# Expert weights loaded in 4 MB pieces of 32 KB per partition, with contraction rows in order 8p+c

## The chip, the cores and the metric

The kernel runs on one core of one Trainium2 chip. The metric is the device time of that core in microseconds (us). All arithmetic is in float32. The engines named below are TensorE (PE, with its weight loads PEld), VectorE (DVE), ScalarE (ACT), GpSimd (POOL) and SyncE (SP). SP issues nearly all loads; they run on 16 DMA engines that the queues of SP and ACT share.

## The reference, cut to what matters

Two transformer blocks are computed on 256 tokens of width 1024. The first ends in a mixture of 32 experts, of which each token takes 4. Each expert has three matrices of 1024x1024 floats (4 MB each), and every one is read once: 32 x 3 x 4 MB is 403 MB of the 537 MB that the kernel reads.

```python
def expert_block(args):
    xe, e = args
    gate = jnp.minimum(xe @ w_gate[e] + b_gate[e], SWIGLU_LIMIT)
    up = jnp.clip(xe @ w_up[e] + b_up[e], -SWIGLU_LIMIT, SWIGLU_LIMIT)
    act = (up + 1) * (gate * jax.nn.sigmoid(SWIGLU_ALPHA * gate))
    return act @ w_down[e] + b_down[e]
```

Ahead of it stand a modulation (`h * (1 + scale) + shift`, whose shift and scale come from `silu(c) @ w_ada + b_ada`), attention and a router. The second block (three kinds of attention and a dense feed-forward) follows it.

## The kernel before

**Places for weights.** Weights stand in SBUF in slots of 4096 words per partition (16 KB, 2 MB over 128 partitions). Six of them are the tensor `ring`. In the expert stage two more, in `arena` (words 13312 on), make it a rotation of `MRING = 8`, and one block (`ASIDE`, number 3) has a place of its own once. `moe_ring`, `moe_block` and `moe_loaded` (L417 to L433) give slot and semaphore of a block.

**Blocks.** A matrix of an expert is two blocks, its halves by contraction rows. In a block, partition p holds four rows that stand together in memory: `block_load` (L531) reads rows 512 x half + 4p + c. So one load of 2 MB is 128 pieces of 16 KB, each contiguous at both ends. There are 192 blocks: 32 experts x 3 matrices x 2. `weight_block` (L449) numbers the 24 blocks of a group of four experts in the order in which they are used: gate(1), up(1), down(0), gate(2), up(2), down(1), gate(3), up(3), down(2), gate(4), down(3), up(4), where 4 is the first expert of the next group. The last group ends with down(3).

**Loads.** All are issued on SP, in order of use. `first_loads` (L550) brings the blocks 0 to 13 of the first group; those in `EARLY` (9 to 13) come in halves of 1 MB (8 KB per partition), each when a half of a block before it has been read. `expert_load` (L536) brings the rest: for each half SP waits until TensorE has used the block whose slot comes free (`X["used"]`), then issues 2 MB.

**TensorE.** `halves` (L2304) waits for a block's load and then does 8 matmuls, four chunks c of contraction rows times two halves g of the 512 output columns, into the two 64-partition halves of one bank. A float32 matmul is two instructions, so a block is 16 rows of the profile at L2318. `w[:, c, 512 * g:512 * g + 512]` is the moving operand, 512 words in one run. The stationary operand is the gathered tokens (`xeT`) or the turned activations (`actT`). So that chunk c of `xeT` holds rows 512 x half + 4p + c, the normed tokens are turned back in that order by `turn_back` (L2244) into `hperm`, and the modulation's shift for them (parts 6 and 7 of `w_ada`) is gathered with a step of 4 (`mod_transpose` and `mod_sums`, L1972 and L1981).

**A group.** `group_pe` (L2408) runs gate, up and down of each expert with the turning of activations (`act_transpose`, L2358), the gather of the next group's tokens (`gather`, L2294) and the combination into the residual (`combine`, L2379) between. `last_expert` does the last down and combine. The second block's weights follow on the same SP queue.

Of the kernel before, what the change touches and what calls it, by code (L numbers as in the profile page):

```python
# [17 lines left out]
ACT = mybir.ActivationFunctionType  # L18
AX = mybir.AxisListType

P = 128
# [78 lines left out]
def two_blocks(nc, t, out):  # L100
    ctx = ExitStack()
    with ctx:
# [160 lines left out]
        hperm = area(1024, 2048).rearrange("p (t h c d) -> p t h c d", t=TT, h=2, c=4)  # L263
# [148 lines left out]

        def moe_place(k):

            return k if k < ASIDE else k - 1

        def moe_ring(s):  # L417

            return None if s in (4, 5) else (W_MOE + (s if s < 4 else s - 2)) % RING

        def moe_block(k):
            if k == ASIDE:
                return area(7680, SLOT).rearrange("p (c n) -> p c n", c=4)
            s = moe_place(k) % MRING
            r = moe_ring(s)
            a = ring[:, r * SLOT:(r + 1) * SLOT] if r is not None else area(13312 + SLOT * (s - 4), SLOT)
            return a.rearrange("p (c n) -> p c n", c=4)

        def moe_loaded(k):

            s = MRING - 1 if k == ASIDE else moe_place(k) % MRING
            r = moe_ring(s)
            return sem(f"extra_loaded{s - 4}") if r is None else loaded[r]  # L433

        def moe_loads(k):

            s = MRING - 1 if k == ASIDE else moe_place(k) % MRING
            r = moe_ring(s)
            before = 0 if r is None else len(range(r, W_MOE, RING))
            return before + (2 if k == ASIDE else moe_place(k) // MRING + (2 if s == MRING - 1 else 1))  # L440
# [50 lines left out]
        def _(sp_):  # L491
# [38 lines left out]

            def block_load(X, g, q, m, half, k):  # L531
                src = t[("w_gate", "w_up", "w_down")[m]][bass.ds(g * EG + q, 1), half * 512:half * 512 + 512, :]
                sp_.dma_start(moe_block(k).rearrange("p c n -> p (c n)"),
                              src.rearrange("e (p c) n -> p (e c n)", c=4)).then_inc(moe_loaded(k), 16)
# [2363 lines left out]
```

## Time and profile before

| | us |
|---|---|
| median of 3 runs | 1765.93 |
| lowest and highest run | 1765.34, 1766.4 |
| span of the profiled execution | 1763.2 |
| TensorE busy in the span | 1642.3 |
| DMA queue of SP, share of 16 engines | 74.2% |

The profiled execution is listed by its span, from the first instruction to the last. The runs' median lies 2.7 us above it; that part lies around the span. The page is read from its second part (the span in 40 slices, with busy shares and the DMA rate) to its fourth (the chain of work that ended last). The expert stage runs from about 320 us to about 1232 us. In the first 320 us stand the modulation, the projections and attention, in the last 530 us the second block.

### The profile page before, as it was taken

To read this page: it belongs to the slowest core of one execution; us is meant where nothing else is said; L and a number is where in the kernel's file an instruction comes from. 1 tells how busy PE (TensorE), PEld (TensorE's weight loads), DVE (VectorE), ACT (ScalarE), POOL (GpSimd) and SP (SyncE) were. 2 spreads that over 40 slices of the span, in tenths; PEclk is the share of its full clock that TensorE was granted. 3 is DMA by queue.
4 is the path that set the end of the run, shared out by engine and by line. 5 is a ranking of instruction groups with operands and counts; after the bars stand their busy time and mean duration, and the time that the engine had idled before them with its cause. 6 is when DMAs were issued, how large, how long until landed. Compare 5 with 4: busy or idle time off the path is not lost.

```text
span 1763.2 us, 19000 instructions
## 1 busy us (share of the span) xinstructions
PE 1642.3 (93%) x7244; PEld 889.6 (50%) x7244; DVE 730.1 (41%) x1324; ACT 282.9 (16%) x623; POOL 25.2 (1%) x30
## 2 busy tenths in 40 slices
PE   5999999999999798898997988998999999999998
PEld 3567786534333242332322423332676878888743
DVE  2785532332324223233232232332234663777755
ACT  3123450301010010100100101000243334010000
POOL 0210000000000000000000000000000000000000
PEclk9999999999999999999999999999999999999999
DMA  9795235899999999999999999999624334344440
GB/s 381 285 344 165 96 111 206 341 431 429 430 430 430 430 429 430 430 431 429 430 430 430 429 430 430 430 427 418 217 97 142 128 112 144 143 173 162 152 182 24
DMA packets 86255, 537.21 MB, mean 305 GB/s; under 512 B 6160, under 2 KB 7568, under 8 KB 59952
## 3 DMA queue, kind: packets, MB, share of 16 engines
q1 hardware_dynamic: 82384, 530.60, 74.2%
q10 hardware_dynamic: 3808, 5.78, 0.9%
q8 instruction: 39, 0.64, 0.1%
q14 instruction: 24, 0.20, 0.0%
HBM read 535.31 MB, written 1.05 MB: 304 GB/s over the span
## 4 chain that ended last, share of the span: by engine, by line
PE 68%; DMA 25%; DVE 4%; DVEq 1%; issue 1%; ACT 1%; POOL 0%; ACTq 0%; SPq 0%
PE ps L2318 22%; PE ps L1939 22%; DMA ring<-in_w_up 12%; DMA ring<-in_w_gate 10%; PE ps L2659 6%; PE ps L2851 5%; PE ps L2294 3%; PE ps L2379 2%; DMA arena<-in_w_down 2%; DMA ring<-in_w_ada 2%; PE ps L2762 1%; DVE arena L1159 1%; PE ps L2175 1%; PE ps L2093 1%; PE ps L2358 0%
## 5 line engine op out<-in xcount | busy, mean ns | idle before, releaser
L2318 PE MATMUL ps<-ring,arena 128*64 128x512 f32 x2288 | 514.8, 598 | 51.8 <-DMA ring<-in_w_gate 21.4
L2318 PEld LDWEIGHTS ps<-ring,arena 128*64 128x64 f32 x2288 | 161.6, 138 | 387.0 <-issue 317.3
L1939 PE MATMUL ps<-arena,ring 128*128 128x256 f32 x896 | 199.9, 381 | 0.3 <-ACT arena L786 0.3
L2318 PE MATMUL ps<-arena 128*64 128x512 f32 x784 | 179.0, 602 | 11.5 <-DMA arena<-in_w_up 5.7
L1939 PEld LDWEIGHTS ps<-arena,ring 128*128 128x128 f32 x896 | 168.4, 190 | 33.1 <-issue 6.8
L1939 PE MATMUL ps<-ring,arena 128*128 128x512 f32 (+1 forms) x480 | 162.9, 494 | 1.5 <-ACT arena L903 1.3
L858 ACT ACTIVATE arena<-ps 128x512 f32<-128x512 f32 x32 | 19.1, 597 | 670.2 <-PE ps L2358 670.2
L1939 PEld LDWEIGHTS ps<-ring,arena 128*128 128x128 f32 x480 | 90.2, 190 | 64.1 <-issue 56.1
L2318 PEld LDWEIGHTS ps<-arena 128*64 128x64 f32 x784 | 55.8, 138 | 120.5 <-issue 104.0
L1444 DVE TENSOR_TENSOR arena<-ps,arena 128x512 f32<-128x512 f32 x32 | 22.1, 691 | 202.0 <-PE ps L2318 202.0
L1469 DVE TENSOR_TENSOR arena<-ps,g_moe 64x512 f32<-64x512 f32 x32 | 21.9, 683 | 187.0 <-PE ps L2318 187.0
L1454 DVE TENSOR_TENSOR arena<-ps,arena 128x512 f32<-128x512 f32 x32 | 22.1, 691 | 185.9 <-PE ps L2318 185.9
L2379 PE MATMUL ps<-arena 128*128 128x512 f32 x128 | 66.7, 653 | 19.3 <-DVE xres L1479 19.3
L2659 PE MATMUL ps<-ring 128*128 128x256 f32 x256 | 60.4, 384 | 1.6 <-ACT g_moe L990 1.4
L2294 PE MATMUL ps<-arena 128*128 128x256 f32 x256 | 57.7, 383 | 0.3 <-DVE arena L1427 0.3
L2851 PE MATMUL ps<-ring,arena 128*128 128x512 f32 x128 | 56.7, 592 | 0.0
L1939 PE MATMUL ps<-ring 128*128 128x256 f32 x256 | 56.6, 379 | 0.0
L2294 PEld LDWEIGHTS ps<-arena 128*128 128x128 f32 x256 | 47.9, 190 | 13.0 <-issue 6.5
L2659 PEld LDWEIGHTS ps<-ring 128*128 128x128 f32 x256 | 47.3, 190 | 10.9 <-ACT g_moe L990 4.0
L1939 PEld LDWEIGHTS ps<-ring 128*128 128x128 f32 x256 | 48.1, 190 | 6.2
L2379 PEld LDWEIGHTS ps<-arena 128*128 128x128 f32 x128 | 22.1, 196 | 54.8 <-DVE xres L1479 36.8
L624 POOL TENSOR_TENSOR stat<-stat 128x1 f32<-128x1 f32 (+2 forms) x25 | 24.8, 994 | 1733.0 <-DVE stat L1080 1530.9
(351 smaller groups left out, 1562.3 us busy)
## 6 DMA issues: line engine op xcount, KB each, us to landing
ring<-in_w_up SPq DMA_DIRECT2D x54, 2048.0 KB, 33.8
ring<-in_w_down SPq DMA_DIRECT2D x54, 2048.0 KB, 32.0
ring<-in_w_gate SPq DMA_DIRECT2D x47, 2048.0 KB, 33.6
ring<-in_w_in SPq DMA_DIRECT2D x23, 2048.0 KB, 8.4
arena<-in_w_down SPq DMA_DIRECT2D x17, 2048.0 KB, 32.0
arena<-in_w_up SPq DMA_DIRECT2D x16, 2048.0 KB, 30.8
arena<-in_w_gate SPq DMA_DIRECT2D x15, 2048.0 KB, 30.8
ring<-in_w_ada SPq DMA_DIRECT2D x12, 2048.0 KB, 17.2
```

The lines of the kernel that those rows point to most:

```text
L624: pool.tensor_tensor(a, a, stat[:, 240:240 + a.shape[1]], ALU.pow).then_inc(sem("root_done"), 1)
L858: act.activation(actT, bank(3).rearrange("p (c f s) -> p c f s", c=4, f=2), ACT.Copy).then_inc(X["tr_read"], 1)
L1159: last = dve.scalar_tensor_tensor(acc, w[:, j, :], cs_t[:, j, 0:1], acc, ALU.mult, ALU.add)
L1444: dve.tensor_tensor(gbuf, bank(0), bias[:, 0:512], ALU.add).then_inc(X["gate_read"], 1)
L1454: dve.tensor_tensor(ubuf, bank(1), bias[:, 512:1024], ALU.add).then_inc(X["up_read"], 1)
L1469: dve.tensor_tensor(y[r0:r0 + CAP, 0:512], bank(2)[0:CAP, :], g_moe[0:CAP, 0:512], ALU.mult)
L1939: last = pe.matmul(dst, a, b, start=k == 0, stop=k == len(terms) - 1)
L2294: last = pe.matmul(bank(4 + r % 2)[:, T * jj:T * jj + T], hperm[:, tt, j // 4, j % 4, :], S4[:, tt].rearrange("p e s -> p (e s)"), start=t ...
L2318: mm = pe.matmul(dst[CAP * g:CAP * g + CAP, :], stationary(half, c), w[:, c, 512 * g:512 * g + 512], start=half == 0 and c == 0, stop=half ...
L2379: pe.matmul(bank(b), WST[:, P * (2 * pr + tt):P * (2 * pr + tt) + P], ypair[:, pr, 512 * h:512 * h + 512], start=True, stop=True).then_inc ...
L2659: last = pe.matmul(dst, a[:, j, :], b[:, j, :], start=n in (1, 2, 7) and j == 0, stop=j == 3, skip_group_check=n not in (1, 2, 7))
L2851: last = pe.matmul(bank(P_BANK[n]), a, b, start=i == 0 and c == 0, stop=i == 7 and c == 1)
```

## The change

A full matrix (4 MB) becomes one load. In it partition p holds the eight rows 8p to 8p+7, 32 KB in one piece in memory, and it fills two neighbouring slots. The rotation is laid so that these pairs are neighbours: the arena's two slots become numbers 5 and 6, and pairs begin in the slots `PAIRED_AT = (1, 3, 5, 7)`. SP waits for both slots of a pair before it issues. The first 18 blocks (`PAIRED`) and the last two still come as loads of 2 MB: rows 8p + 4 x half + c, 16 KB of each 32 KB. That leaves 172 blocks in 86 loads of 4 MB.

In the first blocks the physical slots are filled in the same sequence and behind the same waits as before, but since slots have other numbers, what they hold differs: block 5 now comes fourth instead of second.

The contraction index of a half is now 8p + 4 x half + c. For gate and up the output columns must come out in that order too, for down to find them. So the moving operand of gate and up takes runs of 4 words with a step of 8 words, `w.rearrange("p c (f g a) -> p c g f a", g=2, a=4)[:, c, g]`; down's stays in one run. `hperm`, the router's weights, the bias table and the shift follow the same order. The bias table is loaded twice as wide (4 DMAs of 256 KB instead of 128 KB) into the place where `hperm` comes later, and POOL copies what is needed out of it; `hperm` and the first bias wait for these copies. The shift's parts 6 and 7 are each turned by 8 matmuls with one output column, where before part 6 was 4 transposes and part 7 was 4 matmuls.

The core of the diff:

```diff
-            def expert_load(X, u, g, q, m, last=False):
+            def expert_load(X, u, g, q, m, last, start):
                 k = weight_block(q, m, last)
-                for half in range(2):
-                    sp_.wait_ge(X["used"], u * GROUP_BLOCKS + (X["before"] - MRING + k + half + 1))
-                    block_load(X, g, q, m, half, k + half)
+                if (start and k < PAIRED) or (last and (q, m) == (EG - 1, 2)):
+                    for half in range(2):
+                        sp_.wait_ge(X["used"], u * GROUP_BLOCKS + (X["before"] - MRING + k + half + 1))
+                        block_load(X, g, q, m, half, k + half)
+                    return
+                sp_.wait_ge(X["used"], u * GROUP_BLOCKS + (X["before"] - MRING + k + 2))
+                sp_.dma_start(moe_pair(k), matrix(g, q, m).rearrange("p c n -> p (c n)")).then_inc(moe_loaded(k), 16)
...
+                    by_rows = w.rearrange("p c (f g a) -> p c g f a", g=2, a=4)
                     for c in range(4):
                         for g in range(2):
+                            moving = w[:, c, 512 * g:512 * g + 512] if m == 2 else by_rows[:, c, g]
                             mm = pe.matmul(dst[CAP * g:CAP * g + CAP, :], stationary(half, c),
-                                           w[:, c, 512 * g:512 * g + 512], start=half == 0 and c == 0,
-                                           stop=half == 1 and c == 3)
+                                           moving, start=half == 0 and c == 0, stop=half == 1 and c == 3)
...
+                if n == 6:
+                    for j in range(KC):
+                        last = pe.matmul(bank(mod_bank(n))[0:64, j:j + 1], src[:, j:512:KC], cst(C_ROW0, 1), start=True, stop=True)
...
+                if n == 7:
+                    for j in range(KC):
+                        last = pe.matmul(dst[64:128, j:j + 1], src[:, j:512:KC], one, start=True, stop=True)
...
+            pool.wait_ge(sem("bias_in"), 64)
+            for g in range(2):
+                rows = slice(64 * g, 64 * g + 64)
+                pool.tensor_copy(btab[rows].rearrange("p (m f c) -> p m f c", m=2, c=4),
+                                 btab_in[rows].rearrange("p (m f g c) -> p g m f c", m=2, g=2, c=4)[:, g]
+                                 ).then_inc(sem("bias_in"), 1)
```

**SP, the loop over groups.** These are the first loads of a turn of the loop: gate(1), up(1), and with the change down(0) too. ISA and REGISTER_ALU rows keep the counters. Before:

```order
L533 ISA [waits block_used]
L533 DMA ring<-in_w_gate 128x4096
L540 REGISTER_ALU
L533 ISA [waits block_used]
L533 DMA arena<-in_w_gate 128x4096
L540 REGISTER_ALU
L533 DMA arena<-in_w_up 128x4096 [waits block_used]
L540 REGISTER_ALU
L533 DMA ring<-in_w_up 128x4096 [waits block_used]
```

Now:

```order
L569 ISA [waits block_used]
L569 DMA ring<-in_w_gate 128x8192
L568 REGISTER_ALU
L569 DMA arena<-in_w_up 128x8192 [waits block_used]
L568 REGISTER_ALU
L569 ISA [waits block_used]
L569 DMA ring<-in_w_down 128x8192
```

One load of 8192 words per partition, behind one wait, stands where two of 4096 with a wait each stood.

**TensorE, the last parts of the modulation at about 105 us.** L1978 and L1990 turn parts 6 and 7 of the modulation (the arena's tile is the part, `stat` holds the ones). Before:

```order
L1939 MATMUL ps<-ring,arena 128x512 x8
L1978 MATMUL ps<-const,arena 128x128 x4
L2032 MATMUL ps<-const,arena 128x128 x4
L1990 MATMUL ps<-stat,arena 128x1 x4
L1939 MATMUL ps<-ring,arena 128x512 x8
```

Now:

```order
L1977 MATMUL ps<-ring,arena 128x512 x8
L2017 MATMUL ps<-const,arena 64x1 x8
L2077 MATMUL ps<-const,arena 128x128 x4
L2031 MATMUL ps<-stat,arena 64x1 x8
L1977 MATMUL ps<-ring,arena 128x512 x8
```

Four transposes and four matmuls became eight and eight matmuls, with stationary operands of 64 columns at a step of 8 words instead of 128 columns at a step of 4. Their place between the two projections is the same.

**POOL, from the first roots to the expert stage.** Its roots feed the norms; the last pair (128x1 x2) is the one of the norm ahead of the experts. Before:

```order
L624 TENSOR_TENSOR stat<-stat 128x1 x4
L624 TENSOR_TENSOR stat<-stat 128x2 x4
L624 TENSOR_TENSOR stat<-stat 128x8 x9
L624 TENSOR_TENSOR stat<-stat 128x1 x2
L474 TENSOR_LOAD npass
```

Now:

```order
L649 TENSOR_TENSOR stat<-stat 128x1 x4
L649 TENSOR_TENSOR stat<-stat 128x2 x4
L649 TENSOR_TENSOR stat<-stat 128x8 x9
L659 COPY arena<-arena 64x1024 x2
L649 TENSOR_TENSOR stat<-stat 128x1 x2
```

The two copies of the bias table, of 1024 words on 64 partitions each, stand ahead of the pair of roots.

## Rows read from the trace of the kernel before

**Rows 1.** The page's second part: DMA busy in tenths and its rate, 40 slices.
```profile
DMA  9795235899999999999999999999624334344440
GB/s 381 285 344 165 96 111 206 341 431 429 430 430 430 430 429 430 430 431 429 430 430 430 429 430 430 430 427 418 217 97 142 128 112 144 143 173 162 152 182 24
```

**Rows 2.** Stretches: length, busy us by engine (instructions), granted clock, DMA share, GB/s.
```profile
624.50:741.60 117.10, 104.38 (x454) 38.02 (x452) 35.05 (x54) 8.85 (x17) 0.00 (x0) 0.99 1.01 430
340.00:474.00 134.00, 131.24 (x588) 47.57 (x586) 46.82 (x73) 10.09 (x19) 0.00 (x0) 0.99 1.01 428
```

**Rows 3.** Chain of work that ended last, start, us, what; expert stage.
```profile
334.13 13.88 PE ps L2318 x64
...
474.82 28.91 DMA ring<-in_w_up
...
702.71 35.31 DMA ring<-in_w_up
...
748.83 13.88 PE ps L2318 x64
...
819.84 35.31 DMA ring<-in_w_up
```

**Rows 4.** DMA view of 360 to 1180 us (pieces of 16 KB).
```profile
DMA packets 24194, 352.33 MB, mean 430 GB/s; under 512 B 2689, under 2 KB 2689, under 8 KB 2689
```

**Rows 5.** DMA view of 45 to 65 us (pieces of 2 KB).
```profile
DMA packets 3840, 7.74 MB, mean 387 GB/s; under 512 B 65, under 2 KB 65, under 8 KB 3839
```

**Rows 6.** DMA view of 5 to 25 us (pieces of 8 KB, with ACT's small loads).
```profile
DMA packets 1576, 8.43 MB, mean 422 GB/s; under 512 B 172, under 2 KB 300, under 8 KB 812
```

**Rows 7.** Timeline, end of the expert stage: start, us, engine, line, what [idle before].
```profile
1207.34 3.65 PE L2318 MATMUL ps<-ring,arena 128*64 128x512 f32 x16 [1.15 <-DMA ring<-in_w_up]
...
1212.32 3.65 PE L2318 MATMUL ps<-ring,arena 128*64 128x512 f32 x16 [1.33 <-DMA ring<-in_w_down]
...
1217.05 3.65 PE L2318 MATMUL ps<-arena 128*64 128x512 f32 x16 [1.07 <-DMA arena<-in_w_down]
...
1224.25 3.65 PE L2318 MATMUL ps<-arena 128*64 128x512 f32 x16 [1.24 <-issue]
```

**Rows 8.** Chain of work that ended last, around 105 us.
```profile
105.77 0.47 PE ps L1978 x4
...
106.68 1.76 PE ps L1990 x8
...
115.45 0.60 ACT arena L724
```

**Rows 9.** Timeline of the weight loads there (L1990 first with step 4, then in one run).
```profile
106.41 1.94 PEld L1990 LDWEIGHTS ps<-stat,arena 128*128 128x128 f32 x8
...
115.79 0.97 PEld L1990 LDWEIGHTS ps<-stat,arena 128*128 128x128 f32 x8 [0.18 <-issue]
```

**Rows 10.** DMA view of 350 to 370 us: issues, median us to landing.
```profile
ring<-in_w_gate SPq DMA_DIRECT2D x2, 2048.0 KB, 13.4
```

**Rows 11.** DMA view of 300 to 330 us: the same.
```profile
ring<-in_w_up SPq DMA_DIRECT2D x1, 2048.0 KB, 7.6
```

**Rows 12.** Line 533: least, median, most us from issue to landing.
```profile
DMA to landing us min/median/max: 7.6/32.3/36.0
```

**Rows 13.** Timeline of SP: the fourth and two later issues.
```profile
305.33 0.33 SPq L533 DMA_DIRECT2D ring<-in_w_up  x1
...
365.96 3.76 SPq L533 DMA_DIRECT2D ring<-in_w_up  x2
```

**Rows 14.** Timeline of ACT's queue: the last three bias loads.
```profile
260.77 1.40 ACTq L808 DMA_DIRECT2D arena<-in_b_all  x3
```

**Rows 15.** Timeline of POOL between 250 and 300 us.
```profile
253.63 1.64 POOL L624 TENSOR_TENSOR stat<-stat 128x8 f32<-128x8 f32 x1 [133.71 <-DVE stat L1080]
299.64 0.56 POOL L624 TENSOR_TENSOR stat<-stat 128x1 f32<-128x1 f32 x1 [44.38 <-DVE stat L1080]
```

**Rows 16.** Timeline of VectorE: an operation over 1024 columns.
```profile
121.30 1.23 DVE L1240 TENSOR_TENSOR arena<-ring 128x1024 f32<-128x1024 f32 x1
```

More of the change, by code:

```diff
@@ L429, in moe_loaded, with moe_area @@
-        def moe_loaded(k):
-            s = MRING - 1 if k == ASIDE else moe_place(k) % MRING
-            r = moe_ring(s)
-            return sem(f"extra_loaded{s - 4}") if r is None else loaded[r]
-        def moe_loads(k):
[L437 to L440, printed above, removed]
+        def moe_area(s, slots=1):
+            r = moe_ring(s)
+            return area(13312 + SLOT * (s - 5), SLOT * slots) if r is None else ring[:, r * SLOT:(r + slots) * SLOT]
@@ new lines, in earlier_loads, with half_loads @@
+        def earlier_loads(k):
+            r = moe_ring(moe_slot(k))
+            return 0 if r is None else len(range(r, W_MOE, RING))
+        def moe_loads(k):
+            s = moe_slot(k)
+            return earlier_loads(k) + (2 if k == ASIDE else moe_place(k) // MRING + (2 if s == MRING - 1 else 1))
+        PAIRED_AT = (1, 3, 5, 7)
+        LAST_BLOCK = N_EXP * BLK_EXP - 1
+        HALF_LOADS = [k for k in range(PAIRED) if k != ASIDE] + [LAST_BLOCK]
+        def half_loads(k):
+            here = [n for n in HALF_LOADS if moe_slot(n) == moe_slot(k)]
+            return earlier_loads(k) + here.index(k) + 1, len(here)
@@ new lines, in first_loads @@
+                order = {4: (1, 0), 6: (1, 1), 8: (0, 2), 10: (2, 0), 12: (2, 1)}
+                for n in (4, 6, 7, 5, 8, 9, 10, 11, 12, 13) if first else range(4, 14):
+                    (q, m), half = order[n - n % 2], n % 2
+                    if not first:
+                        sp_.wait_ge(X["used"], u * GROUP_BLOCKS + (X["before"] - MRING + n + 1))
+                    elif n == 6:
+                        sp_.wait_ge(sem("merged_done"), 4)
+                    elif n in (4, 5, 8):
+                        sp_.wait_ge(X["used"], W_MOE - RING + {4: 4, 5: 5, 8: 6}[n])
+                    elif n in EARLY:
+                        src = t[("w_gate", "w_up", "w_down")[m]][q:q + 1, :, :].rearrange("e (p c) n -> p (e c) n", c=KC)
+                        sp_.wait_ge(sem("half_used"), EARLY.index(n) + 1)
+                        sp_.dma_start(moe_block(n)[:, 0:2, :], src[:, 4 * half:4 * half + 2, :]).then_inc(early_in(n), 16)
+                        sp_.wait_ge(X["used"], X["before"] - MRING + n + (n > 11))
+                        sp_.dma_start(moe_block(n)[:, 2:4, :], src[:, 4 * half + 2:4 * half + 4, :]).then_inc(moe_loaded(n), 16)
+                        continue
+                    block_load(X, 0, q, m, half, n)
+                    if n == 8:
+                        if first:
+                            sp_.wait_ge(sem("wo_done"), 4)
+                        block_load(X, 0, 0, 1, 1, ASIDE)
@@ L2302, in gather, with halves @@
                     gather_round(X, it, r)
-            def halves(X, u, q, m, dst, stationary, last=False, between=None):
+            def halves(X, u, q, m, dst, stationary, last=False, between=None, start=None, passed=None):
                 for half in range(2):
@@ L2406, in down_bias, with group_pe @@
                               stop=True).then_inc(sem("bd_done"), 1)
-            def group_pe(X, it, u, last, first=False):
-                gate(X, it, u, 1)
+            def group_pe(X, it, u, last, first=False, start=None):
+                gate(X, it, u, 1, start)
                 if first:
```

179 lines of the change are left out of this document (86 added, 93 removed).

## The prediction

> **What bounds the kernel now.** I read the page's second part first. From slice 9 on the DMA rate stands at 429 to 431 GB/s for 18 slices, beside 96 to 381 ahead of it and 24 to 217 behind it [rows 1]: in the expert stage the load engines, and nothing else, are full all the time. The stretches say the same: from 340 to 474 us the DMA share is 1.01 with TensorE nearly full (131.24 of 134.00 us), and in one group of four experts the share is 1.01 with TensorE 12.7 us short of full (117.10 - 104.38) [rows 2]. The chain of waits then says which of the two ends last. Up to 474 us it runs through TensorE's matmuls, since the first blocks were there in advance; from 474.82 on its long pieces are loads [rows 3]. Their ends stand one group apart: 819.84 + 35.31 less 702.71 + 35.31 is 117.13 us for 24 blocks, 4.880 us each. TensorE does a block in 13.88 / 4 = 3.47 us when nothing holds it [rows 3]. So the stage ends when the bytes are in: its length is blocks times 4.880 us from the moment (340 us) at which the queue is full, and then a short tail of TensorE work behind the last landings [rows 7].
>
> **The load rate, the term that is meant.** 24194 - 2689 = 21505 pieces of 16 KB and 2689 / 16 = 168 loads land in 820 us [rows 4], again 4.88 us for 2 MB. In a stretch that is as full, with pieces of 2 KB, the rate is 387 GB/s [rows 5], 5.42 us for 2 MB. An engine moves 64 pieces for 2 MB there and 8 here, so a piece costs (5.42 - 4.88) / 56 = 9.6 ns beyond its bytes. Pieces of 8 KB at 422 GB/s [rows 6] are 4.97 us for 16 pieces, which would be (4.97 - 4.88) / 8 = 11 ns; ACT's small loads are in that stretch, so it bounds from above and agrees. At 32 KB an engine moves 4 pieces for 2 MB: 4 x 9.6 = 0.038 us less, 4.842 us. 172 blocks come in pairs: 172 x 0.038 = **6.6 us less**. Ends: nothing, if the piece is cut again on the way or the 9.6 ns don't hold from 16 KB up, and 172 x 8 x 9.6 ns = 13.2 us, if all that pieces cost went. I take 6.6, since three sizes lie on one line.
>
> The Trainium skill ("DMA: Bandwidth & Descriptors", section on where 436 GB/s comes from) puts the ceiling of the ports at 435.2 GB/s. By that, as an estimate, 2 MB takes at least 4.819 us and the gain ends at 172 x 0.061 = 10.5 us; the rows' 430 GB/s stand 1.2% below it.
>
> **Does the queue stay full with half as many, larger loads?** SP now waits for two slots. In the steady part a load lands 32.3 us (median) after its issue [rows 12], so the wait for one more block (3.47 us) leaves over 25 us of queued work: nothing lost. The thin place is the start. The first pair is block 18, issued one block later than now, with the second of the two issues that the row at 365.96 us holds, so at 365.96 + 3.76 - 0.33 = 369.4 instead of 365.96 [rows 13]. Loads issued at 350 to 370 us land after 13.4 us [rows 10] where a lone one takes 7.6 [rows 11], so some 6 us of work are queued, against 3.5 us of delay: still nothing lost, but this is the place where it could be, at most 3.5 us once.
>
> **The tail.** The last three landings of the stage each end a wait: second half of up(3), both halves of down(2) [rows 7]. Before, the first half of down(2) was done at 1212.32 while the second was coming, and 3.65 us of TensorE stood behind the landing at 1217.05. As one load, both halves wait for that same landing, and 3.65 + 3.47 us stand behind it. What follows (combination, then down(3) at 1224.25, whose start the timeline puts down to no load) moves with it. down(3)'s own halves then land in time, as the load engines are not delayed. **3.5 us more.** Bounds: 0, if something else holds down(3) back that long (nothing in the rows does), and 3.5.
>
> **The modulation.** At 105 us the chain runs through TensorE: 0.47 us for the four transposes of part 6 and 1.76 us for the 8 instructions of part 7, then a projection that ACT waits for at 115.45 [rows 8]. All of this is on the path to everything behind it, the filling of the slots too. Now there are 2 x 8 matmuls of two instructions, 32 in all, each with a stationary operand of 64 columns. Such an instruction is as long as its weight load: 0.97 / 8 = 0.12 us for 128 columns in one run, 1.94 / 8 = 0.24 at step 4 [rows 9], and 0.22 us in the pace of the chain. With half the columns and every word still by itself I take half, 0.11 us: 32 x 0.11 = 3.5 us, less 2.23, is **1.3 us more**. Ends: if a strided half costs no more than half of a run (0.06), 1.9 - 2.2 = -0.3; if the step of 8 doubles once more (0.22), 7.0 - 2.2 = 4.8.
>
> **Edits that I cost at nothing, and what hides them.** The bias loads are twice as many bytes, 0.5 MB more at about 262 us [rows 14], about 1.3 us of DMA time where the rate is far from full [rows 1]. POOL's copies may begin at about 266 us and have to end before its root at 299.64 [rows 15]: 33 us for two. The only rows of POOL are roots, 1.64 us for 8 columns and 0.56 for one [rows 15], 0.15 us a column more; 1024 columns at that price would be 158 us each and delay all by some 280 us, while VectorE goes over 1024 columns in 1.23 us [rows 16]. Since a root is a power and this a copy, I take a few us; up to 16 us each it is free. `hperm` waits for it and adds nothing if it isn't late. Block 5 comes fourth, issued at 305.33 [rows 13] and there 7.6 us later [rows 11], 313; TensorE comes to it three blocks after 334.13 [rows 3], at 344.5. The moving operand's new step is free while TensorE keeps its pace; see the rivals.
>
> **The sum.** -6.6 + 3.5 + 1.3 = -1.8 us: a span of 1761.4 for 1763.2, and with the 2.7 us around the span 1764.1 against the median 1765.93. I forecast no change that can be told: about 0.2%, 3.5 us, is what a measurement of this kernel can tell.
>
> **Rivals.**
> 1. *The pieces give more.* If also the spacing between loads or the rest of the per-piece cost goes and the modulation's step costs nothing: -10.5 to -13.2 + 3.5 + 0 is -7 to -10, 1756 to 1759. For it: the 430 GB/s are flat over 18 slices [rows 1], so what limits is systematic. Against: the line through three sizes leaves only half of it to take. A middle case (-8 + 3.5 + 0) gives 1761.4. Together 0.25.
> 2. *The piece is cut again, or the line is flat from 16 KB up.* Then only the costs are left: 3.5 + 1.3 = 4.8 slower, 1770.7; this is also the case in which the change doesn't do what it says. It turns to slower, by what can be told, where the gain of the pieces is under 4.8 - 3.5 = 1.3 us, a fifth of what I take. For it: no row has a piece above 16 KB. 0.18.
> 3. *Reading slows, for a wider pitch in HBM.* Pieces of neighbouring partitions stand 32 KB apart instead of 16, in the 2 MB loads with gaps. 1% of rate is 172 x 0.049 = 8.4 us; with the costs 13 us slower, 1779. For it no row: the pieces in the stretch of [rows 5] stand 24 KB apart (a row of `w_ada` is 6144 words) and fit the line with those 16 KB apart. The Trainium skill (the same page, "Latency and other measured facts") tells of a large drop for row pitches that are big powers of two, with 207 GB/s at 512 KiB; nothing there is as small as 32 KB, and no run here shows it yet. 0.06.
> 4. *The moving operand's step slows TensorE.* At step 4 a weight load takes twice as long as in one run [rows 9]. If gate and up took twice as long, a group would be 16 x 3.47 = 55.5 us more against 12.7 us of slack [rows 2]: 43 us a group, some 300 us in all, 2070. It decides from 12.7 / 55.5 = 23%. Against: those are single words at a step, these are runs of four, and no row has such runs. Under 23% it costs only at the start, about 1 to 3 us. The Trainium skill ("SBUF — State Buffer", the note on cachelines) has lines of 16 bytes and no penalty while a line is used twice; by it this rival falls. 0.06.
>
> **Chances.** The forecast 0.45, within 3.5 us to either side; rival 1 0.25; rival 2 0.18; rivals 3 and 4 0.06 each. Rival 1's middle case lies 1 us beyond the forecast's edge, and a modulation at its dear end would carry the forecast over the other edge only with a gain below 4.8 us. Faster by over 0.2%: 0.25. Within: 0.45. Slower: 0.30. The range takes in rivals 1 and 2 and rival 2 with the dear modulation (3.5 + 4.8 = 8.3, 1774): 1757 to 1775; outside are the far end of rival 1 and rivals 3 and 4, under 0.2.
>
> **What would show it.** In the expert stage: pieces in the DMA view halved, and 116.2 us between the same loads of two groups (4.842 x 24) instead of 117.13; 117.1 speaks for rival 2, more for 3. At the end, two blocks of TensorE (7.1 us) in one piece behind the landing of down(2). At 105 us, the two groups of matmuls 3.5 us together. A block of gate or up at 3.47 us; if not, rival 4. POOL's copies over before 299 us. The prediction is wrong if a group's period is off by more than 0.5 us (4 us over the stage) or if a stretch of the first 340 us has a wait that isn't there now.

## The result, and the profile of the changed kernel

| | before | changed |
|---|---|---|
| median of 13 runs, us | 1765.61 | 1770.17 |
| lowest and highest | 1763.43, 1768.86 | 1768.46, 1776.16 |
| ratio to before, 95% interval | | 1.0030 (1.0023 to 1.0038) |
| span of the profiled execution | 1763.2 | 1768.0 |

The change made the kernel slower, by 0.3%: 5.3 us by the ratio, 4.6 by the medians. The forecast was 1764.1, no change that can be told. The profiled execution of the changed kernel is 1.8 us shorter than its own time of 1769.8, so spans are compared with spans and times with times. (That difference is 1.8 us in every run listed; of the 2.7 us that the forecast put around the span, 0.9 us is the distance of the profiled execution from the median.)

**The expert stage** has become shorter per block. The first fence is the DMA view of 360 to 1180 us, the second the chain of waits in the same stage (start, us, what). They answer to [rows 4] and [rows 3].

```profile
DMA packets 12503, 354.64 MB, mean 432 GB/s; under 512 B 1392, under 2 KB 1392, under 8 KB 1392
```

```profile
710.07 31.62 DMA ring<-in_w_up
...
756.01 13.88 PE ps L2370 x64
...
826.46 31.64 DMA ring<-in_w_up
```

The pieces are halved (12503 - 1392 = 11111 for 24194 - 2689 = 21505), the rate is 432 for 430 GB/s, and a group takes 826.46 + 31.64 - 710.07 - 31.62 = 116.41 us where it took 117.13. That is 4.850 us a block, 0.030 less than before, and 172 x 0.030 = 5.2 us over the stage. A block of TensorE is still 13.88 / 4 = 3.47 us; two of these four blocks are a gate's, whose moving operand has the new step.

**The modulation.** This is the chain around 105 us, which answers to [rows 8], and below it stretches of TensorE (length, busy, granted clock, DMA share, GB/s).

```profile
104.03 2.01 PE ps L2017 x16
106.04 0.59 PE ps L2077 x4
106.63 2.01 PE ps L2031 x16
108.64 9.89 PE ps L1977 x16
118.54 0.60 ACT arena L756
```

```profile
104.00:106.00 2.00, 2.00 (x18) 1.00 1.05 385
106.00:108.60 2.60, 2.60 (x22) 0.78 1.00 365
108.60:111.00 2.40, 2.40 (x4) 0.50 0.07 21
111.00:114.00 3.00, 3.00 (x5) 0.50 0.73 203
114.00:118.00 4.00, 4.00 (x11) 0.97 0.97 371
```

The same view of the kernel before, for the third stretch:

```profile
108.60:111.00 2.40, 2.40 (x7) 1.00 0.95 306
```

The two groups of 16 one-column instructions and the four between them take 4.61 us. Before, the same place took 0.47 + 1.76 us and 0.44 between, 2.67: 1.94 more. The projection behind them then takes 9.89 us, where [rows 8] leave 115.45 - 108.44 = 7.0. Its granted clock is 0.50, which is 1.2 GHz, from before 108.6 to about 114 us. Before that TensorE did 4.6 us of matmuls, all but the middle four with one output column; in the kernel before the clock stays at 1.00 through the same stretch. So this place costs 4.8 us, and the forecast had 1.3.

**The start of the gather** has a wait that the kernel before hasn't (chain of waits, changed kernel first, then before):

```profile
322.81 0.70 ACT arena L868
323.51 0.14 issue
323.64 5.42 PE ps L2339 x24
```

```profile
318.45 0.42 DVE arena L1427
318.88 0.35 DVEq L1434
319.22 0.04 issue
319.27 5.45 PE ps L2294 x24
```

L868 is ScalarE's last copy into `hperm`. The gather now waits for all four copies (`hp_read` 4); before, it started after three and waited for VectorE's selection. What this wait costs is read from two profiles with no fall of the clock here: from the matmuls of L2233 (L2279) to the gather it is 319.27 - 311.14 = 8.13 us before and 322.79 - 314.49 = 8.30 in experiment 3, 0.17 us more.

**The end of the stage** (chain of waits), which answers to [rows 7]:

```profile
1188.35 29.46 DMA ring<-in_w_down
...
1217.95 7.09 PE ps L2370 x32
1225.04 0.59 PE ps L2407 x4
1225.62 1.72 PE ps L2428 x4
1227.34 1.72 issue
1229.06 7.09 PE ps L2370 x32
```

Two blocks in one piece stand behind the landing of down(2), 7.09 us for 3.65. Down(3) starts at 1229.06 instead of 1224.25, 4.8 us late, and so is the end. Of these, 0.8 us stand ahead of the landing (1217.81 for 1217.00), 3.4 are the second block, 0.1 stands between landing and matmul, and 0.5 is the longer "issue" ahead of down(3) (1.72 for 1.24), which is 1.19 in another execution of the changed kernel. Both kernels take the same time from the end of down(3) on: 1768.0 - 1236.15 = 531.85 us here, 531.86 before. Everything that moved lies ahead of that.

### The profile page after: what moved, and what is told of

Read it like the earlier page. It is cut to its first block, busy times and chain, and to the rows that moved or that the text cites. A ratio compares the mean times of both kernels' runs of the same rounds, so it can differ in the third digit from the quotient of the medians.

```text
span 1768.0 us, 18715 instructions
## 1 busy us (share of the span) xinstructions
PE 1653.2 (94%) x7264; PEld 901.3 (51%) x7264; DVE 730.4 (41%) x1324; ACT 283.4 (16%) x623; POOL 27.3 (2%) x32
## 4 chain that ended last, share of the span: by engine, by line
PE 73%; DMA 21%; DVE 4%; DVEq 1%; issue 1%; ACT 1%; POOL 0%; ACTq 0%; SPq 0%
PE ps L2370 25%; PE ps L1977 22%; DMA ring<-in_w_up 11%; DMA ring<-in_w_gate 7%; PE ps L2709 6%; PE ps L2901 5%; PE ps L2339 3%; PE ps L2428 2%; DMA ring<-in_w_down 2%; DMA ring<-in_w_ada 1%; PE ps L2812 1%; DVE arena L1197 1%; PE ps L2220 1%; PE ps L2407 1%; PE ps L2171 0%
## 5 line engine op out<-in xcount | busy, mean ns | idle before, releaser
L2370 PEld LDWEIGHTS ps<-ring,arena 128*64 128x64 f32 x2288 | 169.5, 140 | 378.2 <-issue 347.9
```

Source lines behind the costliest of these rows:

```text
L2370: mm = pe.matmul(dst[CAP * g:CAP * g + CAP, :], stationary(half, c), moving, start=half == 0 and c == 0, stop=half == 1 and c == 3)
```

## The experiments

Ratios are to runs of the kernel before on the same chip, taken together with the kernel's own; kernels of different groups are compared by their ratios, 0.1% being 1.8 us. A difference of two such ratios has the uncertainty of both, 2 to 3 us either way, also where it is given below as one number.

**1. Old modulation in the changed kernel.**

```diff
-                if n == 6:
-                    for j in range(KC):
-                        last = pe.matmul(bank(mod_bank(n))[0:64, j:j + 1], src[:, j:512:KC], cst(C_ROW0, 1), ...)
+                    for q in range(4):
+                        last = pe.transpose(..., src[:, q:512:4] if n in (6, 7) else ..., ident)
```

> The changed kernel with parts 6 and 7 of the modulation as before (8 strided transposes and 8 one-column sums in place of 32 one-column matmuls), all else as changed. The shift of the second norm then stands in the wrong order of rows, so its values are wrong; the work on every engine from there on is the same. Theory A (working theory, from the two traces): the 32 one-column matmuls cost about 1.9 us more than what they replace (4.6 against 2.7 in the chain of waits), and the projection right behind them runs at a lower granted clock and takes 2.9 us longer (9.89 against 6.99), so this kernel is about 4.8 us faster than the changed one, near 1765.4, and its first projection block after the modulation shows 7.0 us again. Theory B: the clock fall behind the modulation is that execution's own accident; then only 1.9 us come back, 1768.3, and the projection shows about 9.9 us here or 7 us in other executions of the changed kernel too. Theory C: something later in the first 340 us (an event at a fixed time) absorbs the modulation's delay, and nothing comes back: within 0.5 us of the changed kernel.

Measured: 2717 us, because the wrong shift sends tokens to other experts and the kernel adds a second pass over them. Only the first 1200 us can be read. The projection behind the modulation takes 6.99 us and its clock is 1.00. The pair up(3) of the second group lands at 622.73 where it landed at 625.30, 2.6 us earlier, although this execution had two falls of the clock (at 34 and at 88 us) that the changed kernel's has not.

**2. New modulation in the kernel before** (the reverse edit).

> The kernel before with only the new modulation parts 6 and 7 (32 one-column matmuls); the shift stands in the wrong order, so its values are wrong, the work is the same. Theory A: slower than the kernel before by 1.9 us for the instructions and by up to 2.9 us for the clock behind them: 1768.5 to 1770.5, with the projection behind the modulation near 9.9 us. Theory B: +1.9 us alone, 1767.5, the projection stays near 7 us. My forecast of this step was +1.3 us.

Measured: also two passes, so again the profile alone.

```profile
110.33 9.72 PE ps L1942 x16
...
309.20 6.87 PE ps L1942 x16
```

The chain has 9.72 us for the projection, and at 309.20 us it is 4.76 us later than the kernel before at the same instruction (304.44). The 1.94 us of instructions and the 2.73 us of clock are 4.67 of these. So the cost comes with this edit alone, and the 1.3 us of the forecast is refuted.

**3. Down(2) of the last group in two loads.**

```diff
+        LAST_HALVED = ((EG - 2, 2), (EG - 1, 2))
-                if (start and k < PAIRED) or (last and (q, m) == (EG - 1, 2)):
+                if (start and k < PAIRED) or (last and (q, m) in LAST_HALVED):
```

> The changed kernel with the last but one matrix of the pass (down of expert 2 in the last group) also in two loads of 2 MB, so that TensorE can start on its first half one block time earlier. Theory A: the end waits for nothing else, so 3.5 us (one block of 16 matmuls, 3.47 us) come back: 1766.7, and the last chain shows 3.6 us x16 behind each load again. Rival: the last landing itself sets the end, in place of the block queue on TensorE (two landings, 4.85 us apart, against 3.47 us of work): then less than 1 us comes back.

Measured: 1767.71 us, 1.0010 (1.0001 to 1.0019), against 1.0030: 3.5 us come back, as theory A said, but the chain doesn't look as either theory said. It no longer waits for down(2) at all:

```profile
1180.81 26.47 DMA ring<-in_w_up
1207.28 0.14 issue
1207.41 13.95 PE ps L2371 x64
```

Four blocks run through from the landing of up(3), which is still one load. Experiment 13 goes on from there.

**4. The pairs with pieces of 16 KB.**

```diff
-                sp_.dma_start(moe_pair(k), matrix(g, q, m).rearrange("p c n -> p (c n)"))
+                sp_.dma_start(moe_pair(k).rearrange("p (h w) -> p h w", h=2),
+                              w[...].rearrange("e (h p c) n -> p (e h) (c n)", h=2, c=4))
```

> The changed kernel with each 4 MB load cut into two pieces of 16 KB per partition from two places (contraction rows in the old order 512h+4p+c for these loads, which gives wrong values but the same bytes and instructions); the number of loads stays as changed. Theory A (size of a piece sets the rate): the period of a group goes back from 116.41 to 117.13 us and the run is about 5 us slower than the changed kernel, 1775, with twice the packets. Rival (number of loads and semaphores sets it, not the pieces): the period stays at 116.4 us and the time at 1770. If a wider spread of the addresses cost rate in the changed kernel, the period here would fall below 116.4.

Measured: 1775.38 us, 1.0057 (1.0044 to 1.0071), 4.8 us over the changed kernel's ratio. In its chain the same load of two groups:

```profile
711.71 31.86 DMA ring<-in_w_up
828.83 31.86 DMA ring<-in_w_up
```

117.12 us, the period of the kernel before to 0.01. With loads of 4 MB and half as many semaphores, but pieces of 16 KB, nothing of the gain is there. The size of a piece makes it, not the number of loads: theory A.

**5. The kernel before with pieces of 8 KB.**

```diff
-                sp_.dma_start(moe_block(k)..., src.rearrange("e (p c) n -> p (e c n)", c=4))
+                sp_.dma_start(moe_block(k)..., src.rearrange("e (h p c) n -> p (e h) (c n)", h=2, c=2))
```

> The kernel before with each expert load of 2 MB cut into pieces of 8 KB per partition instead of 16 KB (rows of the contraction in another order, so values are wrong). One more point on the line of piece sizes. If a fixed time per piece is the cost: 16 KB to 32 KB took 0.030 us off a 2 MB block for 4 pieces fewer per DMA engine, 7.5 ns each, so 8 more pieces add 0.06 us to the block's 4.880, the period of a group becomes 118.6 us and the run about 10 us longer. If the small gain of 32 KB came from something else, the period stays near 117.1.

Measured: a single time of 1775.94 us, about 10 us over before, and this chain:

```profile
829.79 31.99 DMA ring<-in_w_up
948.36 31.99 DMA ring<-in_w_up
```

118.57 us a group, 118.6 expected. Three sizes in full stretches of the same stage now give 4.940, 4.880 and 4.850 us for 2 MB with 16, 8 and 4 pieces per engine: 7.5 ns a piece between each two. The forecast's 9.6 ns came from the 2 KB pieces of another stretch [rows 5] and was a quarter too high; between those 2 KB and 8 KB it is (5.42 - 4.94) / 48 = 10 ns a piece, so one line doesn't hold down to 2 KB.

**6. First 14 blocks from unbroken regions** (source rows as before, all else as changed).

> The changed kernel with the first 14 blocks of the pass taken from the rows that the kernel before takes them from (each 2 MB from one unbroken region, in place of 16 KB at a pitch of 32 KB); sizes, counts and waits of the loads stay as changed, and the values of the first group's products are wrong. Theory A: the pitch costs nothing and the time stays within 1 us of the changed kernel's 1770.17; what the start loses comes from the later arrival of TensorE. Rival (a wider pitch in HBM slows the first loads): 1.5 to 2 us come back, 1768.4, and the rate of 335 to 355 us goes from 352 back to 400 GB/s.

Measured: 1771.07 us, 1.0037 (1.0023 to 1.0051), no gain; the rival's 1768.4 would be 1.0016. The rate of 335 to 345 us was 338 GB/s and of 345 to 355 us 411, but the same stretches differ as much between profiles of kernels with the same loads there (352 and 352 in the changed kernel, 403 and 422 in experiment 8). The pitch of 32 KB is not what costs at the start, and the 4 MB loads, which have no gaps, run faster than before; rival 3 has nothing for it. The Trainium skill ("DMA: Bandwidth & Descriptors", "Latency and other measured facts") tells of a large drop for row pitches at big powers of two; no run here shows one at 32 KB.

**7. Part 7 the old way, part 6 the new way** (one group of 16 one-column instructions).

> The changed kernel with part 7 of the modulation by the 4 strided one-column sums of before and only part 6 by 16 one-column matmuls; values of the shift are wrong, which brings a second pass, so only its profile up to 300 us is read. If every such group takes clock from what follows, the projection behind takes 8 to 9 us and the granted clock of 100 to 120 us lies between 0.83 and 1.00; if it takes both groups, the projection takes 7.0 us.

Measured, from its profile up to 300 us: the projection takes 9.96 us, the granted clock is 0.50 from 108.6 to 114 us. One group, with the eight strided sums of part 7 behind it, takes the whole clock. Neither expectation (8 to 9 us, or 7.0) held; halving the number of such instructions is no mend.

**8. The shift put in order by four small transfers** (modulation on TensorE as before).

```diff
+            for h in range(2):
+                for half in range(2):
+                    act.dma_start(shift_new[64 * h:64 * h + 64, 4 * half:4 * half + 4],
+                                  shift_old[half:P:2, 4 * h:4 * h + 4])
```

> The changed kernel computing the same, with parts 6 and 7 of the modulation on TensorE as before (8 transposes with a step of 4 and 8 one-column sums), and the shift put into the order 8p+c by four small transfers between two SBUF tiles, issued by ScalarE behind the bias loads, long before the shift is read. Theory A (one-column matmuls cost 1.9 us and the lower granted clock behind them 2.9 us): near 1765.4, the changed kernel's 1770.17 less 4.8, the granted clock of 100 to 120 us is 1.00, and the projection behind the modulation takes 7.0 us. Theory B (the clock fall at 110 us is bought back by one elsewhere, so only the instructions count): near 1768.2. The run of this edit with wrong values had a pass more, so its time said nothing; its landing of up of expert 3 in the second group came 2.6 us before the changed kernel's, with falls of the clock at 20 to 40 and 80 to 100 us that the changed kernel's profile doesn't have.

Measured: 1773.34 us, 1.0053 (1.0039 to 1.0067), 4 us slower than the changed kernel where 4.8 faster was expected. The early part did what it should: clock 1.00, projection 6.99 us, and the last group's down(2) was in at 1212.56 instead of 1217.81. All of it is lost behind that. Its chain there:

```profile
1222.08 1.23 issue
1223.31 1.07 PE ps L2368 x2
1224.38 4.61 issue
1228.99 8.74 PE ps L2368 x30
```

TensorE does two instructions of down(3), stands for 4.61 us with nothing that the profile shows to wait for, and does the other 30 at a clock that has fallen (granted 0.58 from 1229 to 1233 us; 8.74 + 1.07 us for 7.09). Just ahead of this place the program jumps over the code of the second pass.

**9. Both mends together.**

> Both mends together, computing the same: the shift put in order by four small transfers, and down of expert 2 of the last group in two loads of 2 MB. Theory A: near 1762 (1765.4 less 3.5), that is 0.2% faster than the kernel before: of the pieces' gain of 5.1 us about 1 us is lost at the start of the full queue and the rest stays. Theory B (the start of the queue or the clock takes more): 1765 or above, no different from before.

Measured: 1771.12 us, 1.0033 (1.0021 to 1.0045), and the same gap at the same two instructions, 4.69 us, followed by 10.09 us for 30 instructions. Neither theory had this gap.

**10. The same two kernels with 16 more instructions in TensorE's program.**

```diff
-            pe.wait_ge(sem("vec_in"), 32)
+            for _ in range(33):
+                pe.wait_ge(sem("vec_in"), 32)
```

(32 waits written make 16 instructions.)

> The kernel with the shift put in order by four small transfers (the one that came out at 1773.34, later than the changed kernel, though its last expert block landed 5.3 us earlier), and 16 more semaphore instructions at the head of TensorE's program (waits on a semaphore that is already up, under an idle time), so that its later code stands where it stands in the changed kernel. Theory A: the gap of 4.61 us after the second matmul of down of expert 3, behind the jump over the second pass's code, is TensorE waiting for its own instructions, because the target of the jump lies close to the end of a piece of code; moved by 16 instructions the gap goes, and with it the 1.65 us that the following 30 matmuls lost at a lower clock: 1773.3 less 4.6 less 1.6, near 1767. Rival: the gap comes from the data of that stage (the down bias, the other engines), and stays at 4.6 us: 1773.

> The same padding with both mends (shift by transfers, down of expert 2 of the last group in two loads), computing what the reference computes. Theory A: 1771.1 less 4.7 for the gap and less 3.0 for the clock behind it: near 1763.5, 0.1% faster than the kernel before. Rival (gap from data): 1771.

Measured: 1768.12 us, 1.0017 (1.0008 to 1.0026), and 1764.80 us, 0.9999 (0.9990 to 1.0008). Both are theory A's within 1.3 us. The chain of the first, from down(2) to down(3):

```profile
1217.82 8.71 PE ps L2369 x32
...
1227.12 1.72 PE ps L2427 x4
1228.84 1.35 issue
1230.19 7.09 PE ps L2369 x32
```

The gap is gone and down(3) runs at full clock. A fall there is all the same, one block earlier: down(2) takes 8.71 us for 7.09 (granted 0.66 from 1217 to 1222 us), and in the kernel with both mends 15.64 for 13.95, where experiments 8 and 9 have none. The data, the loads and the other engines' work are those of experiment 8; only the place of the code differs. That the wait is for the program's own instructions is inferred from this, since the profile names no releaser. What is shown is that 16 idle instructions take some 6 us away (1.0053 to 1.0017 and 1.0033 to 0.9999).

**11. Is the rest chance or program?** Even with both mends the kernel was level with before, and not 5 us faster. Three runs asked whether the falls of the clock in the first 320 us belong to a program.

> The kernel before with nothing but the 16 semaphore instructions at the head of TensorE's program. Theory A: where code stands matters of itself; the falls of the granted clock in the first 100 us, of which the padded kernels show one or two more than the kernel before (1.7 us each), come with the shifted code, and this kernel is 2 to 4 us slower than the kernel before. Theory B: those falls differ from execution to execution, and the time is that of the kernel before within 1 us.

> The changed kernel, once more profiled. If the falls of the clock belong to the program, it shows the same as in the first profile: none at 20 to 40 us, one at 108 us (9.9 us for the projection behind the modulation), one at 315 to 320 us, and the gather starts at 323.6 us. If they belong to the execution, at least one of the three differs, by 1.1 to 1.7 us in the gather's start.

> The kernel before, once more profiled. Falls that belong to the program: one at 20 to 40 us (clock 0.91), none until 307 us, gather at 319.3 us. Falls that belong to the execution: another number of them, and the gather 1.7 us earlier or later.

Measured: the padded kernel before 1768.68 us, 1.0015 (1.0006 to 1.0024). So instructions at the head of the program cost about 2.6 us (1.1 to 4.2; 3.8 by the medians) of themselves, and experiment 10 carried that cost. Theory A's reason isn't seen: the profile has one fall in the first 100 us, as the first one of the kernel before, and its gather starts at 322.00 us, while the next profile, without padding, has 322.07. Where the 2.6 us go stays open. The kernel before, profiled again (1768.65 us), had a fall at 90 us that the first profile has not; its gather started at 322.07 us for 319.27. This is its chain (6.87 us for the 16 in the first profile):

```profile
89.55 1.45 PE ps L1996 x4
91.00 8.22 PE ps L1939 x16
```

The changed kernel again had the falls of its first profile, 9.78 us behind the modulation (1769.18 us). These two profiled executions are 0.6 us apart in their spans (1767.4 and 1766.8) where the first two were 4.8 apart: one pair of profiles can't price this change. Over all 20 profiles of this study, these are the granted clocks of four stretches:

| stretch, us | one-column modulation (8 profiles) | old modulation (12 profiles) |
|---|---|---|
| 33 to 40 | below 1.00 in 2 | below 1.00 in 11 |
| 88 to 100 | below in 1 | below in 5 |
| 104 to 120 | **below in 8 (0.79 to 0.89)** | **below in none** |
| 307 to 340 | below in 6 | below in 3 |

Only the third row is cleanly the work's doing (the 0.89 is experiment 6, whose projection took 8.78 us; in the other seven it took 9.65 to 9.96). The others come and go, the second even between two executions of one program. The Trainium skill ("TensorE: Matmul & The Clock Gate", "What's actually happening") says that the place at which the clock changes varies between runs of the same kernel. Here more than the place varies: the two profiles of the kernel before show one fall and two.

**12. Padding placed late.** The 16 instructions now stand behind the loop over the groups, ahead of the last group.

```diff
                 if first:
                     passes[0] = passes_of(pe)
+                    for _ in range(32):
+                        pe.wait_ge(sem("vec_in"), 32)
```

> Both mends and the 16 semaphore instructions again, but placed behind the loop over the groups, ahead of the last group, where TensorE waits for loads anyway: the code of the first 1100 us stands where it stands in the kernel without padding, whose gather started at 317.7 us, and only the target of the jump moves. Theory A (shifted code costs clock early on): the gap of 4.7 us is gone and the early part stays short: 1761.5 to 1762.5, 0.2% faster than the kernel before and about 2.5 us faster than with the padding at the head (1764.8). Theory B (early falls belong to the execution): no different from 1764.8 within 1 us.

> The changed kernel with the shift put in order by four small transfers (parts 6 and 7 of the modulation as before) and the 16 semaphore instructions ahead of the last group, all else as changed. It takes the one-column matmuls away without moving early code. Theory A (they cost 1.9 us and the clock behind them 2.9 us): 4 to 5 us faster than the changed kernel: 0.05% slower than the kernel before, 1766. Theory B (only 2 us, as the padded run without late placement suggested): 1768.

> The changed kernel with only the 16 semaphore instructions ahead of the last group. A control: the jump of the changed kernel lands on no edge (its gap was 1.7 and 1.2 us), so nothing should move and the run stays within 1 us of the changed kernel, 1770. If the late padding is worth something of itself, it is faster by 2 us, and the gains of the padded kernels belong to it.

Measured:

| kernel | median us | ratio (95%) |
|---|---|---|
| changed, late padding | 1770.25 | 1.0025 (1.0015 to 1.0035) |
| and shift by transfers | 1767.10 | 1.0005 (0.9996 to 1.0014) |
| and down(2) in two loads | 1762.84 | 0.9988 (0.9979 to 0.9997) |

The control stays with the changed kernel, so the late padding is worth nothing where there is no gap. The one-column matmuls then cost 3.5 us against the control, or 4.4 against the changed kernel, between the two theories (1766 and 1768 for 1767.10) and with both inside the uncertainty; down(2) costs 3.0. The third row is faster than both kernels. Against the padding at the head it is 1.9 us faster by the ratios, with intervals that overlap, so theory A's 2.5 us isn't shown; and its reason fails, for the early code is that of experiment 9, whose gather started at 317.67 us with no fall ahead of 100 us, and here the gather starts at 321.12 with two. In the profile of the second row down(2) again took 8.78 us for 7.09.

**13. Up(3) in two loads as well.**

> The kernel with both mends and the late padding (1762.84), and up of expert 3 of the last group also in two loads of 2 MB. In its profile TensorE runs through from the landing of that matrix as one load (1205.56) to the last blocks, so the landing of the pair now sets the end. Theory A: TensorE starts on it 3.5 us earlier and then waits for down of expert 2 again, so only 0.6 us come back: 1762.2. Rival: the whole 3.5 us come back, 1759.3.

Measured: 1761.32 us, 0.9977 (0.9967 to 0.9987), the best of the study. 1.9 us by the ratios, between the two expectations, whose difference the intervals don't settle. The wait for a pair has moved up once more; TensorE runs through from the landing of gate(3), the first 32 instructions at a fallen clock (8.78 us for 7.09):

```profile
1196.11 0.14 issue
1196.25 8.78 PE ps L2369 x32
1205.03 0.59 PE ps L2406 x4
1205.62 13.88 PE ps L2369 x64
```

## Why the forecast was wrong, step by step

| step | forecast, us | measured, us |
|---|---|---|
| pieces of 32 KB | -6.6 | -5.2 (period), -4.8 (experiment 4) |
| start of the full queue | 0 | +0.6 to +2.3 in six profiles, see below |
| tail, down(2) | +3.5 | +3.4 in the chain, 3.0 to 3.5 by the runs |
| modulation | +1.3 | +1.9 instructions, +2.9 clock; 3.5 to 4.4 by the runs |
| other edits | 0 | +0.2 for `hperm`; a fall of the clock at 318 us, +1.0, may belong to them |
| sum | -1.8 | +3.0 of pieces, tail and modulation; +5.3 (4.1 to 6.7) by the ratio |

The two first profiles differ by 4.8 us, which their landmarks share out: the gather starts 4.4 us late (4.8 of modulation and 1.1 at the gather, less the 1.7 of a fall at 34 us that only the kernel before has here; 0.2 is spread), down(2) of the last group lands 0.8 us late, so 3.6 of the period's 5.2 us were won between, and 4.0 us are lost from that landing to down(3).

**What bounds the kernel** was read rightly: the chain waits for loads from 477 us on, and a group lasts as long as its bytes.

**The pieces.** The mechanism was right, the size a quarter too large (6.6 for 5.2 us): the period was forecast at 116.2 us and is 116.41. What was mis-sized is the slope: 9.6 ns came from 2 KB pieces. The pieces of 8, 16 and 32 KB lie on a line of 7.5 ns.

**The queue** stayed full from 355 us on, as forecast, but not at the thin place that the forecast named: from 345 to 355 us the changed kernel's rate is 352 GB/s (share 0.94) for 414 (1.01) before. In experiment 8, whose gather starts at the time of the kernel before (319.35 for 319.27), down(2) of the last group lands 4.4 us earlier, of the 5.2 that the period gives. Counted like this, from the gather's start to that landing and against the first profile of the kernel before, 0.6 to 2.3 us are missing in six profiles with pairs (both of the changed kernel, experiments 8, 10 and two of 12), but 0.8 also in the second profile of the kernel before. How much of it the change makes is open.

**The tail** is the term that came out as written.

**The modulation** is the step that failed, and it is what turned the sign: with 4.8 in place of 1.3 us the forecast's own sum is +1.7. Its instruction price was a little low: 0.11 us was forecast, and 2.01 / 16 is 0.126. With that the term is 1.9 instead of 1.3, within its bounds of -0.3 to 4.8. What the forecast had no term for is what a chain of nearly columnless instructions does to the work behind it: the clock of the next projection at half for some 5.8 us, +2.9 us. It is shown both ways: the fall stands in all 8 profiles with these instructions, experiment 2's among them, and in none of the 12 without. Whether their number, their step or their single column does it, no run separates. Rows of the kernel before didn't show it, because eight such instructions with a step of 4 leave the clock at 1.00 there. The whole place, 4.8 us, happens to be the dear end of the range, though not for the reason given.

**Other edits.** POOL's copies take 2.22 us together and end at about 272.6, long before the root at 302.88. Block 5, the bias loads and the moving operand's step end no wait in the chain. `hperm` does: the gather's start waits for its last copy, 0.17 us, a wait of the kind that the forecast named as a sign of being wrong. A fall of the clock at 318 us (8.30 us from L2279 to the gather in experiment 3, which hasn't got it, and 323.64 - 314.38 = 9.26 in the changed kernel) stands in 6 of 8 profiles of kernels with the one-column modulation and in 3 of 12 others. That it comes with the change is likely by these counts, but nothing took it away by itself; it stays open. One more edit was left out of the account: TensorE's program now has the first group written out ahead of the loop (`group_pe(X, it0, u0, False, start=start)`, then `Fori(1, GROUPS - 1)`), since its waits differ. The profile puts no wait of TensorE between 340 and 1200 us to it, but it moves all later code, and no run took it back.

**The rivals.** Rival 1 (pieces give more) is refuted by the period. Rival 2 named the right time, 1770.7, by luck: the pieces did pay, and what cancels them is the modulation with its clock. Rival 3 is refuted by the shorter period and experiment 6, rival 4 by the 13.88 us for four blocks.

**What stays open.** The best kernel gains 4.0 us, and the pieces alone would give 5. The number of falls in the first 320 us differs between executions, 1.7 us each at 34 and 90 us. The fall at 34 us is absent in both profiles of the changed kernel and present in both of the one before, with the same instructions there, but the code's place doesn't fix it either: it is there in the control of experiment 12, whose early code is the changed kernel's. No run tells what decides it.

## What to carry to other kernels

A gain in the rate of a load-bound stage is its per-piece cost times the pieces saved, and that cost has to be read at piece sizes next to the one in question. What pays for it stands at the stage's ends: keep the last matrices in small loads, since each one loaded whole makes its first block wait for the second. And an edit of a few one-column matmuls on the critical path is priced with the granted clock of what follows, not by its own duration; a reordering of a thousand words is better done by a transfer that nobody waits for.

## What the runs showed of the hardware

- A piece costs 7.5 ns beyond its bytes per DMA engine at 8, 16 and 32 KB alike; the rates are 424, 430 and 432 GB/s. The Trainium skill ("DMA: Bandwidth & Descriptors", "Where 436 GB/s comes from") has a ceiling of 435.2 GB/s for the ports; the trace's 432 is 0.7% below it.
- One-column float32 matmuls with 64 stationary columns at a step of 8 words last 0.126 us each, and 16 of them with the eight strided sums are followed by 3.5 to 7 us at 1.2 GHz (worked out from granted clocks of 0.89 to 0.79 over 104 to 120 us, 8 profiles).
- A moving operand in runs of 4 words at a step of 8 costs nothing: 13.88 us for four blocks, two of them a gate's, as before.
- TensorE can stand 4.6 us after a jump, with two instructions done, and 16 idle instructions ahead of it take that away. The clock falls in the gap, and the block pair then takes 9.81 and 11.16 us for 7.09.
- 16 idle instructions at the head of the program made the kernel before 0.15% (0.06 to 0.24) slower.
